# Two blocks of a network on one core: state of the delta rule in pairs of heads, finer waits, wider value products, last level of the inverse on one quarter

## What is computed

```python
def hybrid_mixer(h, w_in, ...):
    proj = h @ w_in
    aq, ak = apply_rope(aq, cos, sin), apply_rope(ak, cos, sin)
    attn_out = dilated_attention(aq, ak, av)           # causal, per head: softmax(q k^T + mask) v
    qkv = silu(causal_dwconv(dn_qkv, dn_conv_w))       # 4 taps
    dq, dk, dv = split(qkv)
    o = gated_delta_rule(dq, dk, dv, beta, g)
    ...
def gated_delta_rule(q, k, v, beta, g):                # per head and chunk of tokens
    A = where(strict, (k * beta) @ k.T * decay, 0)
    T = inverse(A + I)                                 # unit lower triangular
    u, w = T @ (v * beta), T @ (k * beta * exp(g))
    # from chunk to chunk
    v_new = u - w @ state
    o = q_dec @ state + (q @ k.T * decay) @ v_new
    state = state * g_last + k_dec.T @ v_new
```

## Time and profile before

| | us |
|---|---|
| median of 3 runs | 1928.96 |
| lowest, highest run | 1923.92, 1930.76 |
| the profiled execution, its own time | 1936.42 |
| its span in the profile | 1934.6 |
| PE busy (share of the span) | 1678.4 (87%) |
| DVE busy | 872.2 (45%) |
| ACT busy | 546.1 (28%) |
| POOL busy | 572.2 (30%) |
| mean granted clock of TensorE | 0.945 of full |

### The profile page before, as it was taken

One profiled execution on the slowest core, in us unless ns is written; L12 is line 12 of the kernel. 1 busy time (PEld: TensorE's weight loads), 2 busy tenths in 40 slices (PEclk: granted clock), 3 DMA queues, 4 the chain that ended last, 5 costly groups with the idle time before them and its releaser, 6 DMA issues.

```text
span 1934.6 us, 19045 instructions
## 1 busy us (share of the span) xinstructions
PE 1678.4 (87%) x6306; PEld 1022.7 (53%) x6306; DVE 872.2 (45%) x2136; ACT 546.1 (28%) x1521; POOL 572.2 (30%) x597
## 2 busy tenths in 40 slices
PE   7998988787778877677696999899999999999998
PEld 2545563444434322222242587687775587677775
DVE  1477666655546365646444246332123246322112
ACT  2234324323232323233332235321112135221111
POOL 0000046655564666676664002110000002110000
PEclk9999999988888988899898999999999999999999
DMA  9745169988997999999999331074543331074510
GB/s 355 265 174 206 50 236 393 337 314 323 336 330 278 354 365 360 360 382 407 363 372 376 133 131 44 5 267 160 166 142 109 131 115 60 1 272 134 173 64 22
DMA packets 171255, 438.54 MB, mean 227 GB/s; under 512 B 12291, under 2 KB 58531, under 8 KB 171028
## 3 DMA queue, kind: packets, MB, share of 16 engines
q0 software_dynamic: 81824, 299.99, 41.5%
q1 hardware_dynamic: 89334, 137.33, 20.2%
HBM read 436.23 MB, written 1.05 MB: 226 GB/s over the span
## 4 chain that ended last, share of the span: by engine, by line
PE 56%; issue 32%; DVE 4%; ACT 3%; DMA 2%; another core or an unknown queue 1%; DVEq 1%; SPq 0%; POOL 0%; ACTq 0%
PE psum L1107 14%; PE psum L1118 6%; PE psum L881 4%; PE psum L822 2%; PE psum L791 2%; PE psum L1128 2%; PE psum L792 2%; PE psum L630 2%; PE psum L610 2%; PE psum L805 2%; PE psum L1096 2%; PE psum L1078 1%; PE psum L910 1%; PE psum L513 1%
## 5 line engine op out<-in xcount | busy, mean ns | idle before, releaser
L791 PE MATMUL psum<-arena 128*128 128x512 f32 x512 | 298.7, 668 | 165.5 <-ACT arena L1495 85.7
L2095 DVE CUSTOM_DVE_ANT_0 arena<-arena,psum 128x1024 f32<-128x1024 f32 x224 | 273.6, 1221 | 305.1 <-DMA arena<-in_expert_u,indices 211.9
L1234 POOL DMA_INDIRECT arena<-in_expert_v,indices x256 | 245.6, 959 | 203.1 <-PE psum L792 87.3
L792 PE MATMUL psum<-arena 128*128 128x512 f32 x512 | 282.8, 636 | 0.0
L1107 PE MATMUL psum<-activations_T,weight_ring 128*128 128x256 f32 x1280 | 279.2, 379 | 0.0
L1231 POOL DMA_INDIRECT arena<-in_expert_u,indices x256 | 244.6, 955 | 90.9 <-issue 77.2
L791 PEld LDWEIGHTS psum<-arena 128*128 128x128 f32 x512 | 96.2, 206 | 325.0 <-issue 197.4
L1107 PEld LDWEIGHTS psum<-activations_T,weight_ring 128*128 128x128 f32 x1280 | 243.0, 190 | 39.8 <-issue 7.7
L2327 DVE SCALAR_TENSOR_TENSOR arena<-psum,small,arena 128x254 f32<-128x254 f32 (+1 forms) x176 | 76.8, 478 | 322.2 <-ACT arena L1641 318.6
L1186 POOL TENSOR_TENSOR small<-small 128x1 f32<-128x1 f32 (+4 forms) x29 | 30.5, 1050 | 560.3 <-DVE small L2206 218.0
L792 PEld LDWEIGHTS psum<-arena 128*128 128x128 f32 x512 | 105.5, 206 | 139.1 <-issue 139.1
(11 more groups left out here) (396 smaller groups left out, 2062.9 us busy)
## 6 DMA issues: line engine op xcount, KB each, us to landing
weight_ring<-in_ffn_w_in SPq DMA_DIRECT2D x44, 1024.0 KB, 7.8
weight_ring<-in_w_in SPq DMA_DIRECT2D x15, 2048.0 KB, 12.8
weight_ring<-in_w_ada SPq DMA_DIRECT2D x12, 2048.0 KB, 7.8
arena<-in_ffn_w_out POOLq DMA_DIRECT2D x22, 1024.0 KB, 5.2
weight_ring<-in_w_out SPq DMA_DIRECT2D x6, 2048.0 KB
weight_ring<-in_w_pq SPq DMA_DIRECT2D x4, 2048.0 KB, 10.2
weight_ring<-in_w_in SPq DMA_DIRECT2D x2, 2080.0 KB
arena<-in_expert_u,indices POOLq DMA_INDIRECT x256
```

Source lines behind the costliest of these rows:

```text
L791: mm(o0, DIAG[:, n % ND, :], VROWS[n % NV][:, 0:512], start=m == 0, stop=m == PICKS - 1)
L792: mm(o1, DIAG[:, n % ND, :], VROWS[n % NV][:, 512:1024], start=m == 0, stop=m == PICKS - 1).then_inc(sem("v_used"), 1)
L1234: nc.gpsimd.indirect_dma_start(VROWS[g % NV], None, a["expert_v"], bass.IndirectOffsetOnAxis(ap=where, axis=0)).then_inc(sem(f"v_row{g % N ...
L2095: ttr(out=DOTJ[n >= UNIT], in0=UROWS[n % NU], in1=h2, scale=1.0, scalar=0.0, op0=ALU.mult, op1=ALU.add, accum_out=DOT[:, i, m:m + 1]).then ...
```

## The change

Five edits, each done once per layer.

1. `rot2` counts queries and keys of the second tile apart, and PE waits for each before it turns that one.
2. `cv_silu` is waited for in three steps, two activations for each eight turns.
3. The value products of attention take both heads of a pair at once, as 256 columns that are written as two pieces of 128 of a bank.
4. Level 6 of the inverse has one block that is not zero in each matrix, a corner of 64 by 64. Both its products are done on that corner, from `AT` without a mask. ACT copies 64 partitions by 256 into `TW`, DVE subtracts 64 by 256, and POOL makes no mask for it, so that it makes four masks per layer.
5. The state steps are done for two heads at a time, each pair in its own bank. PE waits for the pair that it needs, DVE copies or subtracts 256 columns at a time, and the last outputs wait per pair.

```diff
@@ PE: attention @@
-                        for e in range(2):
-                            for i in range(2):
-                                for s in range(i + 1):
-                                    ins = mm(o[:, e * SEQ + i * P:e * SEQ + (i + 1) * P], V2[:, s, h * P:(h + 1) * P], EPT[:, h % 2, e, i + s, :], start=s == 0, stop=s == i)
+                        both = o.rearrange("p (e i q) -> p e i q", e=2, i=2)
+                        for i in range(2):
+                            for s in range(i + 1):
+                                ins = mm(both[:, :, i, :], V2[:, s, h * P:(h + 1) * P], EPT[:, h % 2, :, i + s, :], start=s == 0, stop=s == i)
...
-                pe.wait_ge(sem("rot2"), L + 1)
                 for wh in range(2):
+                    pe.wait_ge(sem("rot2"), 2 * L + wh + 1)
...
-                pe.wait_ge(sem("cv_silu"), 6 * (L + 1))
                 m["tq"] = []
                 for wh in range(3):
+                    pe.wait_ge(sem("cv_silu"), 6 * L + 2 * wh + 2)
@@ PE: the inverse @@
-                    else:
-                        pe.wait_ge(sem("am_ready"), 5 * L + lv - 1)
+                    elif lv < 6:
+                        pe.wait_ge(sem("am_ready"), 4 * L + lv - 1)
...
+                        if lv == 6:
+                            ins = mm(o[64:P, h * 64:(h + 1) * 64], AT[0:64, half, h, 64:P], TI[0:64, n, 0:64], start=True, stop=True)
+                            continue
...
-                        ins = mm(o[:, h * P:(h + 1) * P], TW[:, n, :], TU[:, n, :], start=True, stop=True)
+                        ins = mm(o[0:64, h * 64:(h + 1) * 64], TW[64:P, n, 0:64], TU[64:P, n, 64:P], start=True, stop=True)
@@ PE: the state; the four banks of all heads give way to @@
+                def pair(g, stationary, moving):
+
+                    o = bank_d()
+                    for q in range(2):
+                        h = 2 * g + q
+                        ins = mm(o[:, q * P:(q + 1) * P], stationary[:, h, :], moving[:, h * P:(h + 1) * P], start=True, stop=True)
+                    ins.then_inc(d_full, 1)
+                    return c["d"]
+
+                first_done = [pair(g, TU[:, 0:4, :], TQ[:, 2, 0, :]) for g in range(2)]
+                carried = []
+                for g in range(2):
+                    pe.wait_ge(d_free, first_done[g])
+                    carried.append(pair(g, AT[:, 2, :, :], UU[:, 0, :]))
                 o = bank_a()
...
+                second_done = []
+                for g in range(2):
+                    pe.wait_ge(d_free, carried[g])
+                    second_done.append(pair(g, TU[:, 4:8, :], TQ[:, 2, 1, :]))
                 o = bank_a()
                 for h in range(DH):
+                    if h % 2 == 0:
+                        pe.wait_ge(d_free, second_done[h // 2])
@@ POOL @@
-                for lv in range(2, 7):
+                for lv in range(2, 6):
@@ ACT @@
-                        heads_of(TW, half)
+                        if lv < 5:
+                            heads_of(TW, half)
+                        else:
+                            o = full()
+                            act.copy(TW[64:P, 4 * half:4 * half + 4, 0:64], o[64:P, 0:256].rearrange("p (h j) -> p h j", h=4)).then_inc(a_free, 1)
@@ DVE @@
-                ins.then_inc(sem("rot2"), 1)
+                        if i == 1:
+                            ins.then_inc(sem("rot2"), 1)
...
+                        else:
+                            corner = TU[0:64, s, 64:P]
+                            tt(corner, corner, o[0:64, 0:256].rearrange("p (h j) -> p h j", h=4), ALU.subtract).then_inc(d_free, 1)
...
+                pairs = [slice(g * 2 * P, (g + 1) * 2 * P) for g in range(2)]
+                for e in pairs:
+                    o = full()
+                    copy(UU[:, 0, e], o[:, 0:2 * P]).then_inc(d_free, 1)
+                for e in pairs:
+                    o = full()
+                    tt(TQ[:, 2, 1, e], TQ[:, 2, 1, e], o[:, 0:2 * P], ALU.subtract).then_inc(d_free, 1)
+                for e in pairs:
+                    o = full()
+                    copy(UU[:, 1, e], o[:, 0:2 * P]).then_inc(d_free, 1)
```

More of the change, by code:

```diff
@@ L2272, in _ @@
                             continue
-                        T = TI if lv < 6 else TU
                         o = full()
-                        tt(T[:, s, :], T[:, s, :], o.rearrange("p (h j) -> p h j", h=4), ALU.subtract).then_inc(d_free, 1)
+                        if lv < 6:
+                            tt(TI[:, s, :], TI[:, s, :], o.rearrange("p (h j) -> p h j", h=4), ALU.subtract).then_inc(d_free, 1)
+                        else:
+                            corner = TU[0:64, s, 64:P]
+                            tt(corner, corner, o[0:64, 0:256].rearrange("p (h j) -> p h j", h=4), ALU.subtract).then_inc(d_free, 1)
                     if lv == 0:
```

## The result

The changed kernel took 1913.68 us, median of 9 runs (1903.89 to 1923.4), beside 1928.68 for the kernel before (9 runs, 1923.92 to 1930.76). The ratio is 0.9927, with a 95% interval from 0.9908 to 0.9947: 15.0 us or 0.73% faster, and between 10 and 18 us by the interval. Run again on another chip, where the part ahead of the first L822 is 80 to 97 us shorter in the traces, it was 1830.27 (6 runs) against 1839.61 (11 runs), ratio 0.9947 (0.9934 to 0.9960): 9.3 us, 7 to 12. Some of the 15.0 can be scatter of the part that was not edited.

What follows compares the result with a forecast made beforehand. PE's queue with holes was taken as the bound, the clock second. Gains of 7.45 us in the first layer and 5.65 in the second, 13.1 together, took the median 1928.96 to 1915.9 us; range 1909.5 to 1922.5.

Steps and rivals of the forecast that it cites:

- The bound: From the second block's first layer, one PE queue with holes; time won reaches the end; the clock comes second.
- Part 1: PE's wait for rotated queries and keys: eight turns move into the hole, 2.4 us, first layer only; low end 0.8.
- Part 2: PE's wait for convolved columns: turns start after two activations; 1.5 us per layer, a slow stretch partly covered.
- Part 3: Wider value products in attention: 1.30 us instead of 1.34, four per layer, 0.15 us a layer, 0.3 in all.
- Part 4: Last level of the inverse on 64 by 64 corners: 1.6 us less tile-shape changes, 1.2 per layer, ends 0.4 and 1.6.
- Part 5: State steps in pairs: gain 2.2 us in the first layer, 2.8 in the second, where the low clock had lengthened it.
- with the holes mostly filled it need not fall: Second layer's state: the clock could stay high, which would gain 3.5 us; 2.8 was taken.
- The sum: Both layers' edited stretches: 7.45 us in the first and 5.65 in the second, together 13.1 us, giving 1915.9 us.
- The low clock at every one of these places: Rival: the clock is low at all edited places, leaving 6.1 us gain, about 1923 us; chance 0.16.
- won time was not lost behind: Rival claimed the opposite: a transfer or DVE chain ends last in the feed-forward part, about 1929 us; chance 0.06.
- The two-piece output: Rival at the value products: writing two pieces doubles each, 10.4 us more, about 1926 us; chance 0.04.
- serial corner records: Rival at the inverse's last level: corner products run one by one at whole latency, 1941 us; chance 0.03.

## Why the prediction was right, point by point

- **The bound.** Right in the main: PE's queue with holes, in which every us won arrives. The stretches between the edits (54.6 or 54.5 us of convolution, 53.7 from the gate projection to the last level's first turn) did not move. No new wait came behind, but one that was there grew by 0.3 us, at the start of layer 1.
- **Part 1**, 2.4 us: measured 2.5 against the one trace of the kernel before. The 0.9 of moved turns is sure; the rest is a low stretch that the unedited place shows in three of six traces, so the mean over traces is 1.7.
- **Part 2**, 1.5 a layer: measured 2.3 and 1.6 in the change, 0.7 and 1.9 alone. The mean of 12 edited layers against 10 unedited ones with the same gates is 2.1 (8.2 against 10.3), so this term was too small. The slow stretch behind the 8-column products was right; "partly covered by the wait for ACT's copies" holds where one such stretch comes (7.8 to 8.3 us) and not where two do (9.1 and 9.4).
- **Part 3**, 0.3 us: right in the products' own time, and the rule on non-contiguous patterns in "PSUM — Partial Sum Buffer", Specifications (TRN2), of the Trainium skill did not bite: 1.30 us for six records in two pieces of 128 columns each. Of the 0.3, 0.2 arrives.
- **Part 4**, 1.2 a layer: measured 1.4, in the change and alone. Two of the four changes of tile shape show in the chain; the 0.4 that was taken off for them was a little too much.
- **Part 5**, 2.2 and 2.8: measured 2.2 and 3.5 at the state itself. Tile 0's chain did become the later one (L1064 7.5 us behind the first state product, as worked out). The step that failed is "with the holes mostly filled it need not fall". I looked at the state only. In the 12 layers that were traced with the state in pairs and nothing in the hole at its end, the clock was low on the output projection in six (1.7 us each) and on the state in one; in the 12 with the state as before, never on the output projection and on the state in three. The mean gain at the state is 2.5 a layer, the 5.0 of the forecast, and 1.7 of it goes at the output projection.
- **The sum**, 13.1 us: it lies between the two comparisons, 15.0 and 9.3, and inside the interval of the first, above that of the second (7 to 12). The account by stretches gives 2.5 + 3.9 + 0.3 + 2.8 + 5.7 = 15.2; less 3.4 for the two low stretches that came on the output projection and at the start of layer 1, and 0.3 for the longer wait there, that is 11.5, and 11.3 was the difference of the traces. By the means over all traces it is 1.7 + 4.2 + 0.2 + 2.8 + 5.0 = 13.9, less 1.7 at the output projection and 0.9 at the start of layer 1, 11.3 again. So the forecast came near partly by luck: part 2 was too small and part 1 too large, and there was no term for the 2.6 us that are lost behind the edits.
- **The rivals.** The low clock at every one of these places did not come. The won time was not lost behind as that rival had it (a transfer or a DVE chain in the feed-forward part), though a fifth of it was, on PE. The two-piece output and the serial corner records are refuted by their own durations; that the first would double a value product was my own price, for which no row stood.

## What to carry to other kernels

Where one engine's queue is the bound, cost each hole twice: by its length and by what the clock takes back from the work behind it; and look for where the low stretch goes when a hole is closed, not only whether it leaves. Look at what PE streams as well as at its busy share: here 32 records of 8 columns went with a fall of the clock in every layer, holes only in some, and the same records at 128 columns cost no time. See how often a low stretch comes before its whole price goes into a sum: the trace of the kernel before showed one that three of five other traces with the same hole had not. When every edit is below what whole runs can tell, a trace from a fixed event to the end, with the low-clock time beside it, tells them apart.

## What the runs showed of the hardware that I had not expected

- During or right behind 32 records of 8 columns, which hold PE busy by the profile, the granted clock fell to its lower level in 22 of 22 layers; at as many of 128 columns, 0.112 us apart, it did not in 5 of 6.
- Products on opposite 64 by 64 corners of the array run side by side (records of L992 and L1022 start 0.003 to 0.006 us apart, and L1022 ahead of three that stand before it in the queue).
- Four turns of 128 by 128 behind such products take 0.60 us in place of 0.44.
- The first L822 of layer 0 started at 1054 to 1078 us in the traces on some chips and at 972 to 975 in those on two others. On the former, whole runs of one kernel scatter by more than all five edits bring (1925.8 to 1946.2).
